# Forgetting attention inside a decoder layer on one core: softmax tiles turned two steps behind their scores, through six buffers, with the per-head work of two engines laid out anew

## The chip, the core and the metric

The kernel runs on one core of one Trainium2 chip. A core has five engines that run their own instruction streams in order and meet through semaphores: PE (TensorE, matrix products), DVE (VectorE), ACT (ScalarE), POOL (GpSimd) and SP (SyncE, which only issues DMAs here). The metric is the device time of one execution in microseconds (us), the median of several runs.

## What is computed

One layer: attention with a forget gate (16 heads of 64, 1024 tokens, width 1024), LayerNorm, then a mixture of 64 small experts with one shared expert, and LayerNorm again. Only the attention bears on the change:

```
proj = x @ w_in                       # q, k, v and one gate logit per head
c = cumsum(log_sigmoid(f_logit + b_f))            # over tokens, per head
logits = q k^T * scale + c[t] - c[s], causal
p = softmax(logits);  o = p @ v;  y = concat(o) @ w_out
```

## The kernel before

Every fp32 product is made of reduced-precision parts: an operand is split into a high part (`_hi`, a cast by ACT) and the rest (`_lo`, a subtraction by DVE that waits for the cast), and `split_matmul` runs three matmuls (lines 80 to 82).

**Value stage.** PE makes the values of all heads in 16 groups `n`, each copied out by ACT and DVE into `v_out` and stored by SP to `v_scratch`. At `n == 9` it also makes the q and k of head 0 (`project(0, half)`, two halves of 512 tokens, 24 matmuls each). The running sums of the gate, `c_hi` and `c_lo`, are ready at `n == 5`; SP stores them after the last group. POOL then waits for these stores before it sets the rows of ones (semaphore `aug`), and SP, ACT, DVE and PE wait for `aug`.

**Head loop.** Head `h` has 8 query tiles of 128 tokens, steps `t` = 0 to 7. The scores of tile `t` span 128(t+1) keys, cut into pieces of up to 512, the 12 slots: one slot for tiles 0 to 3, two for tiles 4 to 7 (slots 4 and 5, 6 and 7, 8 and 9, 10 and 11). Scores land in three PSUM banks in turn (`slot_banks`). Each slot passes:

1. `scores` (PE, lines 817 to 820);
2. `maxima` (DVE, 1548; with two slots also the minimum of their negated maxima, 1552);
3. `exponentials` (ACT, 1193), after the maxima of the whole tile, into `probs[n % 4]`; each is followed by a read of its row sum;
4. `turns` (PE, 847): transposes of 128x128 blocks into one of two banks (`key_banks`, by `u % 2`), after the exponential, and after `turned_low` has read the bank's content of two entries ago;
5. `turned_high` (ACT, 1204), then `turned_low` (DVE, 1559), which give `pt_hi` and `pt_lo`;
6. `weigh_v` (PE, 868): products with the values, once per half of the tiles.

The list `TURNS` has 14 entries `u`: 12 transposes of slots and two `rows` entries, which spread the reciprocals of the row sums over a bank. Slots of tile 7 are turned in step 0 of the next head, all others one step after their scores. Beside this stands work that is done once per head: `project(h + 1)` (PE) in pieces by `PROJECT[t]`, its weights' splitting (`weights_hi` on ACT, 1165, `weights_lo` on DVE, 1500), `take` (both engines read q and k out of PSUM), `low_values` (ACT, 1212), `normalise` (DVE, 1574 and 1578, which frees a key bank) and `reciprocals` (DVE). No scheduler is at work: the order of the code is the order on each engine.

**End.** In head 15 there is nothing to project; ACT and DVE split `w_out` instead (`split_wo`, one piece in each step from 2 to 7, two afterwards), and the last `weigh_v` and the output projection follow.

## Time and profile before

| what | us |
|---|---|
| median of 3 runs (lowest, highest) | 1902.46 (1892.62, 1911.94) |
| the profiled execution | 1887.1 |
| its span, first to last instruction | 1885.4 |
| value stage behind head 0's projection | 104.8 to 145.3 |
| wait between value stage and head 0 | 145.3 to 160.85 |
| heads 0 to 14, up to step 7's maxima of head 14 | 160.85 to 641.6 |
| head 15 up to its last `weigh_v` | 641.6 to 693.8 |
| output projection, routing, experts, last LayerNorm | 693.8 to 1885.4 |

Times of the profile are counted from the span's start. An engine's busy time is the union of its instructions' times; the granted clock is 1.00 at TensorE's upper level (2.4 GHz) and 0.50 at its lower one (1.2 GHz), a mean in between where a stretch saw both.

### The profile page before, as it was taken

How to read it: one execution, taken by the hardware profiler on the slowest of the kernel's cores; microseconds unless marked ns; L12 is line 12 of the kernel's file. 1: busy time of each engine (PE TensorE's matmuls, PEld its weight loads, DVE VectorE, ACT ScalarE, POOL GpSimd, SP SyncE). 2: the span in 40 equal slices, each digit the busy share in tenths (PEclk: the TensorE clock that was granted, in tenths of full speed). 3: DMA queues.
4: the chain of work that ended last, by engine and by line, in shares of the span. 5: the costliest groups of instructions: out<-in, count | busy, mean ns of one | idle time of the engine just before them, and what ended most of it. 6: DMA issues, size and time to landing. Idle time of an engine off the chain costs nothing.

```text
span 1885.4 us, 31807 instructions
## 1 busy us (share of the span) xinstructions
PE 1650.2 (88%) x8302; PEld 1323.5 (70%) x8303; DVE 1200.7 (64%) x2030; ACT 1017.2 (54%) x1672; POOL 474.1 (25%) x486
## 2 busy tenths in 40 slices
PE   7995888888888859989999999999999999999960
PEld 5894666666676648777877777777777777787740
DVE  3212656556565556885566777777776777787836
ACT  3113545554555443333566676766766676777732
POOL 0000000000000000545144444444344443544420
PEclk9998999999999869889999999999999999999995
DMA  5313222212121214264799999998999899999956
GB/s 178 114 68 76 51 51 47 53 39 62 39 62 34 86 62 171 81 236 138 256 299 286 280 302 358 327 282 264 267 301 291 262 317 320 333 339 333 372 135 263
DMA packets 161508, 369.26 MB, mean 196 GB/s; under 512 B 53040, under 2 KB 73520, under 8 KB 161456
## 3 DMA queue, kind: packets, MB, share of 16 engines
q1 hardware_dynamic: 136272, 284.21, 44.2%
q0 software_dynamic: 25184, 84.39, 17.8%
q8 instruction: 28, 0.46, 0.1%
q14 instruction: 24, 0.20, 0.0%
HBM read 294.39 MB, written 65.77 MB: 191 GB/s over the span
## 4 chain that ended last, share of the span: by engine, by line
PE 46%; DVE 19%; issue 11%; DMA 11%; ACT 9%; POOL 2%; DVEq 1%; POOLq 1%; ACTq 1%; SPq 0%
DMA sums_scratch<-ys,sidx 5%; DVE nm L1548 5%; PE bank L969 4%; PE bank L975 4%; PE bank L972 4%; DVE pt_lo L1559 4%; PE out_ps L1027 3%; PE out_ps L1028 3%; DMA x_rows<-rows_scratch,gidx 3%; ACT probs L1193 3%; PE q_ps L959 3%; PE k_ps L1004 2%; PE k_ps L996 2%; PE k_ps L997 2%; PE bank L80 2%
## 5 line engine op out<-in xcount | busy, mean ns | idle before, releaser
L1778 DVE TENSOR_TENSOR gu_lo<-raw_gu,gu_hi 128x1024 fp32r<-128x1024 f32 x260 | 306.8, 1222 | 20.6 <-ACT gu_hi L1297 20.0
L1297 ACT CAST gu_hi<-raw_gu 128x1024 fp32r<-128x1024 f32 x260 | 252.7, 1048 | 0.0
L969 PE MATMUL bank<-gu_hi,xb_hi 128*128 128x512 f32 x576 | 235.0, 408 | 1.4 <-ACT ex L1289 1.3
L972 PE MATMUL bank<-gu_lo,xb_hi 128*128 128x512 f32 x576 | 227.6, 395 | 0.0
L1559 DVE TENSOR_TENSOR pt_lo<-k_ps,pt_hi 128x512 fp32r<-128x512 f32 (+1 forms) x192 | 100.9, 553 | 139.1 <-ACT pt_hi L1204 138.2
L1193 ACT ACTIVATE probs<-bank,nm 128x512 f32<-128x512 f32 (+3 forms) x128 | 73.9, 579 | 191.8 <-DVE nm L1552 107.6
L1778 DVE TENSOR_TENSOR dn_lo<-raw_dn,dn_hi 128x1024 fp32r<-128x1024 f32 x130 | 154.6, 1209 | 0.5 <-ACT dn_hi L1297 0.5
L641 POOL DMA_INDIRECT sums_scratch<-ys,sidx x64 | 114.2, 1784 | 131.4 <-DMA sums_scratch<-ys,sidx 76.8
L975 PE MATMUL bank<-gu_hi,xb_lo 128*128 128x512 f32 x576 | 146.2, 395 | 0.0
L576 POOL IOTA e<- 128x64 f32 x1 | 0.2, 190 | 550.6 <-DVE xs L1578 550.6
L1297 ACT CAST dn_hi<-raw_dn 128x1024 fp32r<-128x1024 f32 x130 | 129.5, 1046 | 0.0
L847 PE MATMUL k_ps<-ident,probs 128*128 128x128 f32 x576 | 94.5, 295 | 38.0 <-DVE pt_lo L1559 31.1
L969 PEld LDWEIGHTS bank<-gu_hi,xb_hi 128*128 128x128 f32 x576 | 109.5, 190 | 25.8 <-issue 2.5
L975 PEld LDWEIGHTS bank<-gu_hi,xb_lo 128*128 128x128 f32 x576 | 108.0, 187 | 26.4
L80 PE MATMUL q_ps<-xt_hi,wqk_hi 128*128 128x512 f32 x256 | 115.2, 450 | 11.9 <-DVE wqk_lo L1500 11.9
L972 PEld LDWEIGHTS bank<-gu_lo,xb_hi 128*128 128x128 f32 x576 | 108.9, 189 | 22.6
L996 PE MATMUL k_ps<-dn_hi,ht_hi 128*128 128x512 f32 x288 | 122.2, 424 | 1.4 <-ACT ht_hi L1326 1.4
L997 PE MATMUL k_ps<-dn_lo,ht_hi 128*128 128x512 f32 x288 | 117.6, 408 | 0.0
L847 PEld LDWEIGHTS k_ps<-ident,probs 128*128 128x128 f32 x576 | 70.9, 150 | 64.9 <-DVE pt_lo L1559 32.2
L959 PE MATMUL q_ps<-ident,x_rows 128*128 128x128 f32 x576 | 85.6, 295 | 29.8 <-DMA x_rows<-rows_scratch,gidx 24.1
L1318 ACT CAST xb_hi<-q_ps 128x1024 fp32r<-128x1024 f32 x72 | 73.1, 1016 | 67.3 <-PE q_ps L959 67.3
L1782 DVE TENSOR_TENSOR xb_lo<-q_ps,xb_hi 128x1024 fp32r<-128x1024 f32 x72 | 88.1, 1224 | 29.7 <-ACT xb_hi L1318 28.2
(268 smaller groups left out, 4123.8 us busy)
## 6 DMA issues: line engine op xcount, KB each, us to landing
raw_gu<-in_moe_w_gate_dram SPq DMA_DIRECT2D x128, 512.0 KB, 6.7
raw_gu<-in_moe_w_up_dram SPq DMA_DIRECT2D x128, 512.0 KB, 8.4
raw_dn<-in_moe_w_down_dram SPq DMA_DIRECT2D x128, 512.0 KB, 6.6
wqk<-in_fox_w_in_dram SPq DMA_DIRECT2D x66, 128.0 KB, 2.4
v_scratch<-v_out SPq DMA_DIRECT2D x32, 256.0 KB, 2.8
va<-v_scratch SPq DMA_DIRECT2D x16, 512.0 KB, 4.7
xs<-in_x_dram SPq DMA_DIRECT2D x8, 512.0 KB, 7.6
wv<-in_fox_w_in_dram SPq DMA_DIRECT2D x4, 1024.0 KB, 7.6
```

The costliest lines, as they stand in the source:

```text
L80: pe.matmul(out, w_hi, m_hi, start=start, stop=False, skip_group_check=True)
L847: i = pe.transpose(bank[:, j * P:(j + 1) * P], probs[n % 4][:, j * P:(j + 1) * P], ident[:])
L959: i = pe.transpose(ps[:, c * P:(c + 1) * P], v[:, c], ident[:])
L969: i = pe.matmul(o3, xb_hi[s][:, c], g_hi[:, :, c], start=c == 0, stop=False, skip_group_check=True)
L972: pe.matmul(o3, xb_hi[s][:, c], g_lo[:, :, c], start=False, stop=False, skip_group_check=True)
L975: i = pe.matmul(o3, xb_lo[s][:, c], g_hi[:, :, c], start=False, stop=c == DC - 1, skip_group_check=True)
L996: pe.matmul(k_ps[:, r], ht_hi[:, c], d_hi[:, c, r], start=c == 0, stop=False, skip_group_check=True)
L997: pe.matmul(k_ps[:, r], ht_hi[:, c], d_lo[:, c, r], start=False, stop=False, skip_group_check=True)
L1193: a.activation(probs[n % 4][:, 0:w], slot_banks[n % 3][:, 0:w], ACT.Exp, bias=nm[:, t:t + 1], accum_out=ssum[par][:, k, t:t + 1]).then_inc ...
L1297: a.copy(hi, raw).then_inc(S[done], 1)
L1559: dve.tensor_tensor(pt_lo[:, at, :], key_banks[u % 2][:, 0:count * P].rearrange("p (j q) -> p j q", q=P), pt_hi[:, at, :], ALU.subtract).t ...
L1778: dve.tensor_tensor(lo, raw, hi, ALU.subtract).then_inc(S[lo_ok], 1)
```

## The change

- `probs` has six buffers in place of four, and `TURNS` and the new `STEP_TURNS` turn every slot two steps behind its scores: tile 6 in step 0 of the next head, tile 7 in step 1.
- On PE the transposes of a step stand ahead of its pieces of projection; the two `weigh_v` move from steps 2 and 5 to 3 and 7.
- On ACT the `turned_high` of a step stand ahead of its `exponentials`. On DVE the `turned_low` still follow the `maxima`.
- The work done once per head is spread over other steps.
- The gate sums are stored during the value stage (`n == 7`), POOL sets the rows of ones without waiting for any store, the second half of head 0's projection follows the value groups, and the weights of head 1 are split there too.

```diff
+PROBS = 6
...
-TURNS = [("turn", -1, 10), ("turn", -1, 11), ("rows", -1, 0), ("turn", 0, 0), ("turn", 0, 1), ("rows", -1, 1)] + [
-    ("turn", 0, n) for n in range(2, 10)]
-
-PROJECT = [((0, 0, 2), (0, 2, 3)), ((0, 3, 7),), ((0, 7, 8),), ((1, 0, 2),), ((1, 2, 4),), ((1, 4, 5),), ((1, 5, 7),), ((1, 7, 8),)]
+TURNS = [("turn", -1, 8), ("turn", -1, 9), ("turn", -1, 10), ("turn", -1, 11), ("rows", -1, 0), ("turn", 0, 0), ("turn", 0, 1),
+         ("turn", 0, 2), ("rows", -1, 1)] + [("turn", 0, n) for n in range(3, 8)]
+
+STEP_TURNS = [(0, 1), (2, 3), (4, 5), (6,), (7,), (8, 9), (10, 11), (12, 13)]
+
+PROJECT = [((0, 0, 3),), ((0, 3, 6),), ((0, 6, 8),), (), ((1, 0, 3),), ((1, 3, 5),), ((1, 5, 7),), ((1, 7, 8),)]
...
-                    probs = [sb(f"probs{i}", [P, BANK], c=b) for i in range(4)]
+                    probs = [sb(f"probs{i}", [P, BANK], c=b) for i in range(PROBS)]
...
-                    nm2 = sb("nm2", [P, 2], c=b)
+                    nm2 = sb("nm2", [P, TT, 2], c=b)
...
+                if n == 7:
+                    sp.wait_ge(S["c_lo_ok"], 2)
+                    sp.dma_start(c_dram[0], c_hi[:].bitcast(F32)).then_inc(S["c_stored"], 16)
+                    sp.dma_start(c_dram[1], c_lo[:].bitcast(F32)).then_inc(S["c_stored"], 16)
...
-            sp.wait_ge(S["c_lo_ok"], 2)
-            sp.dma_start(c_dram[0], c_hi[:].bitcast(F32)).then_inc(S["c_stored"], 16)
-            sp.dma_start(c_dram[1], c_lo[:].bitcast(F32)).then_inc(S["c_stored"], 16)
             sp.wait_ge(S["c_stored"], 32)
+            sp.wait_ge(S["v_ps"], NVC * TT // 2)
+            load_c(sp, 0, 0)
+            copy_halves(sp, 0, 0, 0)
             for i in range(2):
                 sp.wait_ge(v_stored[i], 32 * NVC * TT // 4)
+            load_v(sp, 0, 0)
+            copy_halves(sp, 0, 0, 1)
             sp.wait_ge(S["wqk_lo_ok"], 3)
             load_wqk(sp, 2, 0)
-            sp.wait_ge(S["aug"], 2)
-            for half in range(2):
-                copy_halves(sp, 0, 0, half)
-            load_c(sp, 0, 0)
-            load_v(sp, 0, 0)
...
-            pool.wait_ge(S["v_ok"], NVC * TT // 2)
-            for i in range(2):
-                pool.wait_ge(v_stored[i], 32 * NVC * TT // 4)
-            pool.wait_ge(S["c_stored"], 32)
             pool.wait_ge(S["v_ps"], NVC * TT // 2)
             for par in range(2):
                 g.memset(qk[par][1][DH:K2, :].bitcast(F32), 1.0).then_inc(S["aug"], 1)
...
                     pe.wait_ge(S["c_lo_ok"], 2)
-                    for half in range(2):
-                        project(0, half, range(DC))
+                    project(0, 0, range(DC))
...
-            pe.wait_ge(S["aug"], 2)
+            project(0, 1, range(DC))
 
             def scores(h, par, t):
 
                 q_both, q_ones, k_twice, k_rest = qk[par]
                 if t == 0:
+                    if static(h) and h < 2:
+                        pe.wait_ge(S["aug"], h + 1)
...
-                    for k, (half, c0, c1) in enumerate(PROJECT[t]):
+                    turns(h, par, STEP_TURNS[t], first)
+                    if t == 3 and not first:
+                        weigh_v(h - 1, 1 - par, 1)
+                    if t == 7:
+                        weigh_v(h, par, 0)
+                    for half, c0, c1 in PROJECT[t]:
                         if not last:
                             project(h + 1, half, range(c0, c1))
-                        if t == 0 and k == 0:
-                            turns(h, par, (0, 1), first)
-                    if t == 1:
-                        turns(h, par, (2, 3), first)
-                    elif t == 2:
-                        if not first:
-                            weigh_v(h - 1, 1 - par, 1)
-                        turns(h, par, (4,), first)
-                    elif t == 3:
-                        turns(h, par, (5, 6), first)
-                    elif t == 4:
-                        turns(h, par, (7,), first)
-                    elif t >= 5:
-                        turns(h, par, (2 * t - 2, 2 * t - 1), first)
-                    if t == 5:
-                        weigh_v(h, par, 0)
...
-            turns(HEADS, 0, (0, 1, 2), ends=True)
+            turns(HEADS, 0, (0, 1, 2, 3, 4), ends=True)
             weigh_v(HEADS - 1, 1, 1)
-            turns(HEADS, 0, (5,), ends=True)
+            turns(HEADS, 0, (8,), ends=True)
...
-                if n in (3, 12):
+                if n == 3:
                     for piece in range(2):
-                        weights_hi(n // 12, piece)
+                        weights_hi(0, piece)
...
-                    if not (static(h) and NS * h + n < 4):
-                        act.wait_ge(S["turned_ps"], NS * h + (n - 3))
-                    a.activation(probs[n % 4][:, 0:w], slot_banks[n % 3][:, 0:w], ACT.Exp, bias=nm[:, t:t + 1],
+                    if not (static(h) and NS * h + n < PROBS):
+                        act.wait_ge(S["turned_ps"], NS * h + (n + 1 - PROBS))
+                    a.activation(probs[n % PROBS][:, 0:w], slot_banks[n % 3][:, 0:w], ACT.Exp, bias=nm[:, t:t + 1],
...
+                    for u in STEP_TURNS[t]:
+                        if TURNS[u][0] == "turn" and not (first and TURNS[u][1]):
+                            turned_high(h, u)
                     exponentials(h, par, t)
-                    if t == 0 and not first:
-                        if left > 1:
-                            weights_hi(h + 1, 1)
-                        turned_high(h, 0)
-                        turned_high(h, 1)
+                    if t == 0 and not first and left > 1:
+                        weights_hi(h + 1, 1)
+                    elif t == 1 and not first:
                         take(h, par, 1)
-                    elif t == 1:
-                        turned_high(h, 3)
-                    elif t == 2:
+                        low_values(h - 1, 0)
+                    elif t == 3:
                         if left > 1:
                             take(h + 1, 1 - par, 0)
-                        turned_high(h, 4)
-                    elif t == 3:
                         if not first:
                             low_values(h - 1, 1)
-                        turned_high(h, 6)
-                    elif t == 4:
-                        turned_high(h, 7)
-                    elif t >= 5:
-                        if t == 6 and left > 2:
-                            weights_hi(h + 2, 0)
-                        if t == 7:
-                            low_values(h, 0)
-                        for u in (2 * t - 2, 2 * t - 1):
-                            turned_high(h, u)
+                    elif t == 6 and left > 2:
+                        weights_hi(h + 2, 0)
...
-            act.wait_ge(S["aug"], 2)
+            act.wait_ge(S["v_ps"], NVC * TT // 2)
             for half in range(2):
                 take(0, 0, half)
+                weights_hi(1, half)
+            for i in range(2):
+                act.wait_ge(v_stored[i], 32 * NVC * TT // 4)
...
-            turned_high(HEADS, 0)
-            turned_high(HEADS, 1)
+            for u in range(4):
+                turned_high(HEADS, u)
+            low_values(HEADS - 1, 0)
...
-                    if t == 0 and not first:
-                        if left > 1:
-                            weights_lo(h + 1, 1)
+                    if t == 0 and not first and left > 1:
+                        weights_lo(h + 1, 1)
+                    if t == 2 and not first:
+                        normalise(h - 1, *before_it, 0)
+                    if t == 5 and not first:
+                        normalise(h - 1, *before_it, 1)
+                    for u in STEP_TURNS[t]:
+                        if TURNS[u][0] == "turn" and not (first and TURNS[u][1]):
+                            turned_low(h, u)
+                    if t == 1 and not first:
                         reciprocals(h - 1, 1 - par, 1)
-                        turned_low(h, 0)
-                        turned_low(h, 1)
                         take(h, par, 1)
-                    elif t == 1:
-                        if not first:
-                            normalise(h - 1, *before_it, 0)
-                        turned_low(h, 3)
-                    elif t == 2:
-                        if left > 1:
-                            take(h + 1, 1 - par, 0)
-                        turned_low(h, 4)
-                    elif t == 3:
-                        if not first:
-                            normalise(h - 1, *before_it, 1)
-                        turned_low(h, 6)
-                    elif t == 4:
-                        turned_low(h, 7)
+                    elif t == 3 and left > 1:
+                        take(h + 1, 1 - par, 0)
+                    elif t == 6:
+                        if left > 2:
+                            weights_lo(h + 2, 0)
                         reciprocals(h, par, 0)
-                    elif t >= 5:
-                        if t == 7 and left > 2:
-                            weights_lo(h + 2, 0)
-                        for u in (2 * t - 2, 2 * t - 1):
-                            turned_low(h, u)
...
             for half in range(2):
                 take(0, 0, half)
+                weights_lo(1, half)
...
-            turned_low(HEADS, 0)
-            turned_low(HEADS, 1)
+            for u in range(4):
+                turned_low(HEADS, u)
+            normalise(HEADS - 1, PAIRS - 1, 1, 0)
             split_wo(range(STAGES, DC))
-            normalise(HEADS - 1, PAIRS - 1, 1, 0)```

ACT, second head of the loop body, steps 6 and 7; `probs`, `pt_hi` and `wqk_hi` are the exponentials, the casts of turned blocks and the weights' high parts. Before:

```order
L1193 ACTIVATE probs0,ssum0<-out_ps,nm 128x512 [waits turned_ps,maxed]
L1193 ACTIVATE probs1,ssum0<-bank0,nm 128x384 [waits turned_ps]
L1161 ISA
L1163 ISA [waits wqk_in0]
L1165 CAST wqk_hi<-wqk 128x512 [waits proj]
L1199 REGISTER_ALU
L1204 CAST pt_hi<-k_ps 128x4x128 [waits pv,turned_ps]
...
L1204 CAST pt_hi<-k_ps 128x2x128 [waits pv,turned_ps]
...
L1193 ACTIVATE probs2,ssum0<-bank1,nm 128x512 [waits turned_ps,maxed]
L1193 ACTIVATE probs3,ssum0<-out_ps,nm 128x512 [waits turned_ps]
```

and now:

```order
L1194 CAST pt_hi<-k_ps 128x4x128 [waits pv,turned_ps]
...
L1194 CAST pt_hi<-k_ps 128x128 [waits pv,turned_ps]
L1178 REGISTER_ALU
L1183 ACTIVATE probs2,ssum0<-out_ps,nm 128x512 [waits turned_ps,maxed]
L1183 ACTIVATE probs3,ssum0<-bank0,nm 128x384 [waits turned_ps]
...
L1155 CAST wqk_hi<-wqk 128x512 [waits proj]
...
L1194 CAST pt_hi<-k_ps 128x4x128 [waits pv,turned_ps]
...
L1194 CAST pt_hi<-k_ps 128x2x128 [waits pv,turned_ps]
...
L1183 ACTIVATE probs4,ssum0<-bank1,nm 128x512 [waits turned_ps,maxed]
L1183 ACTIVATE probs5,ssum0<-out_ps,nm 128x512 [waits turned_ps]
```

The casts of a step moved ahead of its exponentials, and are those of the tile before (slots 4 and 5 in step 6, not 6 and 7).

DVE, end of step 7 of that head and steps 0 and 1 of the next; `pt_lo` is `turned_low`, `nm` the maxima. Before:

```order
L1500 TENSOR_TENSOR wqk_lo<-wqk,wqk_hi 128x512 [waits wqk_hi_ok]
L1559 TENSOR_TENSOR pt_lo<-k_ps,pt_hi 128x4x128 [waits turned_hi]
L1559 TENSOR_TENSOR pt_lo<-k_ps,pt_hi 128x3x128 [waits turned_hi]
L1546 ISA
L1548 TENSOR_REDUCE nm<-bank0 128x1 [waits score]
...
L1500 TENSOR_TENSOR wqk_lo<-wqk,wqk_hi 128x512 [waits wqk_hi_ok]
L1567 TENSOR_TENSOR rsum<-ssum0 128x4 [waits exped]
L1569 RECIPROCAL rec0<-rsum 128x4 [waits rec_step]
...
L1559 TENSOR_TENSOR pt_lo<-k_ps,pt_hi 128x4x128 [waits turned_hi] x2
```

and now:

```order
L1542 TENSOR_TENSOR pt_lo<-k_ps,pt_hi 128x4x128 [waits turned_hi]
L1542 TENSOR_TENSOR pt_lo<-k_ps,pt_hi 128x2x128 [waits turned_hi]
L1529 ISA
L1531 TENSOR_REDUCE nm<-bank0 128x1 [waits score]
...
L1484 TENSOR_TENSOR wqk_lo<-wqk,wqk_hi 128x512 [waits wqk_hi_ok]
...
L1542 TENSOR_TENSOR pt_lo<-k_ps,pt_hi 128x4x128 [waits turned_hi]
...
L1542 TENSOR_TENSOR pt_lo<-k_ps,pt_hi 128x3x128 [waits turned_hi]
L1529 REGISTER_ALU
L1531 TENSOR_REDUCE nm<-bank1 128x1 [waits score]
...
L1542 TENSOR_TENSOR pt_lo<-k_ps,pt_hi 128x4x128 [waits turned_hi] x2
```

The first split of the weights left step 7; the second one in step 0 still stands ahead of that step's `turned_low`, which is now that of tile 6, and tile 7's follows in step 1.

SP, from the last store of values to the first loads of head 0. Before:

```order
L376 DMA v_scratch<-v_out 128x512
L380 DMA c_scratch<-c_hi 16x1024 [waits c_lo_ok]
L381 DMA c_scratch<-c_lo 16x1024
L301 DMA wqk<-in_fox_w_in_dram 128x4x64 [waits v_stored1,wqk_lo_ok,v_stored0,c_stored]
...
L321 DMA q_ones<-q_both 64x512 [waits aug,ev_hi]
L322 DMA k_twice<-k_twice 64x512
...
L307 DMA k_rest<-c_scratch 2x1024
L310 DMA va<-v_scratch 128x8x128
```

and now:

```order
L383 DMA v_scratch<-v_out 128x512
L310 DMA k_rest<-c_scratch 2x1024 [waits v_ps,c_stored]
L324 DMA q_ones<-q_both 64x512 [waits ev_hi]
L325 DMA k_twice<-k_twice 64x512
L313 DMA va<-v_scratch 128x8x128 [waits v_stored1,v_stored0]
L324 DMA q_ones<-q_both 64x512 [waits copied,ev_hi]
```

The stores of the gate sums are gone from here, and the loads that head 0's first scores need come first.

## Rows read from the trace of the kernel before

**Rows 1.** The page's line on DVE's and PE's busy time.

```profile
PE 1650.2 (88%) x8302; PEld 1323.5 (70%) x8303; DVE 1200.7 (64%) x2030; ACT 1017.2 (54%) x1672; POOL 474.1 (25%) x486
```

**Rows 2.** Stretches of the program: length, then busy times, clock, DMA.

```profile
core 0: us, PE busy (x) PEld busy (x) DVE busy (x) ACT busy (x) POOL busy (x), PEclk, DMA share, GB/s
145.30:160.85 15.55, 0.00 (x0) 0.03 (x1) 3.45 (x5) 4.22 (x6) 2.39 (x4) 0.65 0.41 96
160.85:188.50 27.65, 24.28 (x111) 18.26 (x112) 10.35 (x25) 10.64 (x31) 0.00 (x0) 0.89 0.23 57
188.50:641.60 453.10, 392.38 (x2074) 301.02 (x2073) 272.81 (x576) 234.22 (x615) 0.00 (x0) 0.97 0.20 49
641.60:693.80 52.20, 29.19 (x120) 22.04 (x118) 31.23 (x57) 26.61 (x57) 0.00 (x0) 0.63 0.25 86
```

**Rows 3.** Two heads of the loop, then 0.8 us at the start of one.

```profile
382.50:415.00 32.50, 28.64 (x149) 22.04 (x149) 19.60 (x43) 16.77 (x44) 0.00 (x0) 0.95 0.20 49
415.00:447.40 32.40, 27.51 (x148) 20.97 (x148) 19.39 (x41) 16.77 (x44) 0.00 (x0) 1.00 0.20 49
...
386.00:386.80 0.80, 0.80 (x3) 0.61 (x3) 0.00 (x0) 0.78 (x2) 0.00 (x0) 0.50 0.41 89
```

**Rows 4.** Timeline, steps 6 and 7: start, length, instruction [idle before <- releaser].

```profile
410.26 0.39 PE L81 MATMUL q_ps<-xt_lo,wqk_hi 128*128 128x512 f32 x1
410.47 0.68 DVE L1548 TENSOR_REDUCE nm<-out_ps 128x1 f32<-128x512 f32 x1
410.49 0.39 PE L82 MATMUL q_ps<-xt_hi,wqk_lo 128*128 128x512 f32 x1
...
411.06 0.55 DVE L1548 TENSOR_REDUCE nm<-bank 128x1 f32<-128x384 f32 x1
...
411.84 0.69 ACT L1193 ACTIVATE probs<-out_ps,nm 128x512 f32<-128x512 f32 x1 [2.04 <-DVE nm L1552]
...
412.67 0.50 PE L817 MATMUL out_ps<-k_twice,q_both 128*128 128x512 f32 x1 [0.66 <-ACT probs L1193]
...
413.07 0.61 ACT L1165 CAST wqk_hi<-wqk 128x512 fp32r<-128x512 f32 x1
...
413.58 0.86 ACT L1204 CAST pt_hi<-k_ps 128x512 fp32r<-128x512 f32 x2
...
414.21 1.02 DVE L1559 TENSOR_TENSOR pt_lo<-k_ps,pt_hi 128x512 fp32r<-128x512 f32 x2 [2.40 <-ACT pt_hi L1204]
414.95 0.99 PE L847 MATMUL k_ps<-ident,probs 128*128 128x128 f32 x7 [0.71 <-DVE pt_lo L1559]
415.14 0.68 DVE L1548 TENSOR_REDUCE nm<-bank 128x1 f32<-128x512 f32 x1
...
417.32 0.50 PE L80 MATMUL q_ps<-xt_hi,wqk_hi 128*128 128x512 f32 x1 [0.48 <-DVE wqk_lo L1500]
```

**Rows 5.** Timeline, from the value stage to the first scores.

```profile
145.93 0.69 DVE L1531 TENSOR_TENSOR v_out<-bank,v_out 128x512 fp32r<-128x512 f32 x1 [5.06 <-ACT v_out L1179]
146.65 0.81 SPq L376 DMA_DIRECT2D v_scratch<-v_out  x2
...
150.73 1.95 POOL L566 MEMSET q_ones<- 2x1024 f32 x2 [146.49 <-DMA c_scratch<-c_lo]
152.71 0.59 ACT L1184 ACTIVATE q_both<-q_ps 64x512 fp32r<-64x512 f32 x1 [6.81 <-POOL q_ones L566]
...
160.85 0.44 PE L817 MATMUL bank<-k_twice,q_both 128*128 128x128 f32 x1 [15.58 <-DMA k_rest<-c_scratch]
```

**Rows 6.** DMA issues there: KB each, median us to landing.

```profile
k_twice<-k_twice SPq DMA_DIRECT2D x2, 128.0 KB, 2.7
```

**Rows 7.** Timeline, end of head 15.

```profile
684.36 0.68 ACT L1193 ACTIVATE probs<-out_ps,nm 128x512 f32<-128x512 f32 x1
...
686.62 1.06 ACT L1217 CAST wo_hi<-wo 128x1024 fp32r<-128x1024 f32 x1
...
690.69 2.36 DVE L1584 TENSOR_TENSOR wo_lo<-wo,wo_hi 128x1024 fp32r<-128x1024 f32 x2 [0.25 <-ACT wo_hi L1217]
...
693.79 0.77 PE L868 MATMUL out_ps<-pt_hi,va 128*128 128x512 f32 x1 [2.83 <-DVE heads_sum L1574]
```

More of the change, by code:

```diff
@@ L833, in bank_free @@
                     assert u < 2
-                    pe.wait_ge(S["turned_lo"], NS * h + (TURNS[12 + u][2] + 1 - NS))
+                    pe.wait_ge(S["turned_lo"], NS * h + (TURNS[len(TURNS) - 2 + u][2] + 1 - NS))
             def turns(h, par, us, first=False, ends=False):
@@ L846, in turns @@
                         for j in range(SLOTS[n][2] // P):
-                            i = pe.transpose(bank[:, j * P:(j + 1) * P], probs[n % 4][:, j * P:(j + 1) * P], ident[:])
+                            i = pe.transpose(bank[:, j * P:(j + 1) * P], probs[n % PROBS][:, j * P:(j + 1) * P], ident[:])
                         i.then_inc(S["turned_ps"], 1)
@@ L1519, in _ @@
             for n in range(NVC * TT // 2):
-                if n in (3, 12):
+                if n == 3:
                     for piece in range(2):
-                        weights_lo(n // 12, piece)
+                        weights_lo(0, piece)
                 if n and n % (TT // 2) == 0 and n // (TT // 2) + 1 < NVC:
@@ L1532, in _ @@
                                   ALU.subtract).then_inc(S["v_ok"], 1)
-            dve.wait_ge(S["aug"], 2)
             def take(h, par, half):
@@ L1547, in maxima @@
                     one = len(OF_TILE[t]) == 1
-                    dve.tensor_reduce(nm[:, t:t + 1] if one else nm2[:, k:k + 1], slot_banks[n % 3][:, 0:SLOTS[n][2]], AX_X, ALU.max,
+                    dve.tensor_reduce(nm[:, t:t + 1] if one else nm2[:, t, k:k + 1], slot_banks[n % 3][:, 0:SLOTS[n][2]], AX_X, ALU.max,
                                       negate=True).then_inc(S["maxed"] if one else S["max_step"], 1)
@@ L1551, in maxima @@
                     dve.wait_ge(S["max_step"], TT * h + 2 * (t - 3))
-                    dve.tensor_tensor(nm[:, t:t + 1], nm2[:, 0:1], nm2[:, 1:2], ALU.min).then_inc(S["maxed"], 1)
+                    dve.tensor_tensor(nm[:, t:t + 1], nm2[:, t, 0:1], nm2[:, t, 1:2], ALU.min).then_inc(S["maxed"], 1)
             def turned_low(h, u):
@@ L1630, in _ @@
             reciprocals(HEADS - 1, 1, 1)
-            turned_low(HEADS, 0)
-            turned_low(HEADS, 1)
+            for u in range(4):
+                turned_low(HEADS, u)
+            normalise(HEADS - 1, PAIRS - 1, 1, 0)
             split_wo(range(STAGES, DC))
-            normalise(HEADS - 1, PAIRS - 1, 1, 0)
             def heads_lo(t):
```

## The prediction

> **What bounds the kernel now.** I read the busy shares first: PE 88% and DVE 64% of the span [rows 1]. No engine is full, so the stretches decide. Four of them are touched: a wait of 15.55 us with PE idle; head 0; fourteen head-to-head distances, 453.1 us or 32.4 us each; head 15 with 52.2 us [rows 2]. The rest is left alone.
>
> In one head of 32.4 us at full clock PE is busy 27.5 us, DVE 19.4 and ACT 16.8 [rows 3]; PE idles 4.9 us. What ends its waits is read from the timeline of two steps [rows 4]. From the maxima of step 6 (410.47) to those of step 7 (415.14) DVE and ACT work one after the other: two maxima and the minimum 1.37 us, until the exponential starts at 411.84; both exponentials to 413.07, 1.23; the weights' cast to 413.58, 0.51; the casts of the turned blocks until DVE can begin at 414.21, 0.63; DVE's two subtractions to 415.14, 0.93. The sum is 4.67 us, the whole step. DVE idles 2.40 us of it and ACT 2.04, each for the other, and PE, with about 3.0 us of work in the step, stands at 412.67, 414.95 and 417.32 for one or the other. So the bound is a ring: maxima(t), exponentials(t), turned_high, turned_low, maxima(t+1), on two in-order engines.
>
> **The ring goes.** In the new order ACT casts blocks of two tiles ago while DVE is at the maxima, and DVE's turned_low finds its cast done. A step then costs an engine its own work: for DVE in step 6 1.37 + 0.93, with weights and a reciprocal 3.1 us; ACT about the same. PE becomes the longest. Its issue time per head is a little under the 27.5 us busy: a matmul that is followed at once takes 0.23 us of its 0.39 [rows 4], and one ahead of a wait counts in full, 0.16 us for some four or five places, so 26.8.
>
> **What PE still waits for.** I walked one head of the new order by hand with the durations of rows 4, from PE's step 7 as time 0. DVE is 2.4 us behind there, since weights_lo has moved to step 6 and waits for a cast that stands behind that step's exponentials. Maxima of step 7 end at 3.85, exponentials at 5.65, turned_low of slots 6 and 7 at 4.5 and 4.85. PE reaches the next head at 4.0, and its transposes need those two banks: waits of 0.3 and 0.3. In step 0 ACT does two casts (6.6), an exponential (7.1), the weights' cast (7.75); DVE's weights_lo waits for that one (8.5), and only then come turned_low of slots 8 and 9 (9.1, 9.6). PE wants these banks for tile 7 at 7.95 and waits 1.2 us, the largest gap. In step 1 DVE's take waits for ACT (14.0), normalise in step 2 ends at 15.9, and PE's transpose of step 3, which needs its bank, waits 0.5 us. The second weigh_v of a head is then free to start. Steps 4 to 7 show no wait of PE: the score of a tile's second slot comes some 3 us after that of the tile before, and maxima, minimum and exponential take 2.2 of them. The waits make 2.3 us, of which 0.2 overlap; 26.8 + 2.1 = 28.9, and I add 0.3 for semaphore hops that I left out: **29.2 us a head**. Fourteen of them save 14 x (32.4 - 29.2) = **44 us**. The six buffers cost nothing by themselves. Bounds: no wait at all is the 27.5 us row, 69 us saved; waits twice as long, 30.5 to 31.3 us, save 27 to 15.
>
> **The wait ahead of head 0.** Before, PE ends the value stage at 145.3 and starts scores at 160.85 [rows 2, 5]: the last values are stored at 146.65, then the gate sums, POOL waits for their landing and takes 1.95 us, ACT starts at 152.71, the copies and loads follow. Afterwards half of head 0's projection, 24 x 0.23 = 5.5 us, stands behind the value groups, so these end at 139.8 and the projection at 145.3. Meanwhile ACT and DVE take the first half (to 143), POOL fills its rows (to 141.9), and SP, behind two stores of values (0.81 us), loads the sums and issues the copies at about 143.5; with 2.7 us to landing [rows 6] scores start near 146.5. That is **14.4 us** (11 if the copies queue behind the values' stores, 15.5 at most). The store moved to n = 7 passes SP's queue while groups of 5.8 us run, its sums being long ready: nothing. The splitting of head 1's weights fits between the two takes.
>
> **Head 0** ran at a clock of 0.89 [rows 2] because PE came from a long idle: 0.11 of 27.65 us, 3 us. After an idle of one us I expect the upper level. With 1 us more for its last steps, **4 us** (0 to 5).
>
> **Head 15.** There the ring has one more member pair, the split of w_out: ACT's cast 1.06 us and DVE's subtraction, half of 2.36 [rows 7], stand in it in every step from 2 on. They stay, as DVE waits for the cast behind the exponentials; what leaves is the pair of casts of turned blocks, about 0.9 us in seven steps, 6.3 us. At the end, from the last exponential's end (684.36 + 0.68) to the last weigh_v (693.79) it is 8.7 us [rows 7], with 2.36 us of w_out ahead of normalise. The new tail turns four slots instead of two (two of them can start earlier) and puts normalise first; by the same durations 6.0. So 2.7 us more, **9 us** in all (3 to 12).
>
> **The sum.** 44 + 14.4 + 4 + 9 = 71.4 us, from the profiled 1887.1 to 1815.7. The median of the runs is 1902.46, 15.4 us above the profiled one; I put that down to the rest of the program and subtract from the median: **1831 us**. The difference that a measurement of this kernel can tell from none is about 1%.
>
> **Clock.** At a head's start PE fell to 0.50 for some 3 us after gaps of about a microsecond each, in one of two heads: the means are 0.95 and 1.00 [rows 3]. My walk assumes that this stops. The Trainium skill ("TensorE: Matmul & The Clock Gate", section "A second HAM failure mode: psum-queue depth-cycling") describes short idles between groups of matmuls as enough to make the clock swing. The rows of this trace agree with it, and by it the gaps that I leave at the head's start could keep the swing, the third rival below: 1842 by that rule, 1831 by my walk.
>
> **Rivals.**
> 1. PE is the bound with no gaps of note (my lags of DVE are too long): 27.5 us a head, 69 us in place of 44: 1806. For it: ACT and DVE are under 20 us busy. Against: the 1.2 us gap follows from in-order queues. 0.17.
> 2. A new ring at the head's start: ACT's exponentials of step 7, casts, weights' cast, DVE's weights_lo, turned_low, PE's transposes. If every hop is longer than I took, the head costs 30.5 us and the loop saves 27: 1848. 0.15.
> 3. The clock swing stays, 1.6 us in each pair of heads, seven pairs: 11 us: 1842. The idle that is left is half of that before. 0.12.
> 4. The change doesn't do what it says in the loop (PE's transposes ahead of the projections make it wait for the banks in each step), the loop stays at 32.4, and the rest saves 27: 1875. 0.04.
> 5. Slower. The projections were what PE did while its banks were read; now the transposes come first, and each bank is freed by a turned_low behind the maxima of the step. If each of 8 steps showed the wait of step 1 (1.2 us) and PE ran a quarter of the loop at its lower level, the head would be 26.8 + 9.6 + 3.4 = 39.8 us, 104 us more in the loop, less 27 elsewhere: 1980. It decides from 34.3 us a head, 7.5 us of waits against my 2.4. The rows speak against it: DVE would need to be late by a step each time. 0.03.
>
> The forecast has 0.49. The range runs from 1805 (rival 1) to 1858 (rival 2 with the lower bounds of the smaller terms), and leaves out rivals 4 and 5 and edges of the others. Faster by over 1%: 0.95; within 1%: 0.02; slower: 0.03.
>
> **What would show it.** In the new profile the distance of heads is 29 us, PE busy near 27 of them; DVE's idle ahead of turned_low (2.40 in a step) is near zero, save in step 0; PE's largest wait is for turned_low of slot 8 ahead of the transposes of step 1, near 1.2 us; the first scores stand near 146.5; head 15 is some 9 us shorter. I am wrong if PE waits in steps 4 to 7 for exponentials or banks, if its clock mean falls under 0.95 in the loop, or if the first scores still wait for a DMA issued after 150.

## The result, and the profile after

The changed kernel takes 1795.86 us (median of 4 runs, 1792.89 to 1798.77); the kernel before, timed beside it on the same chip, 1902.33 (4 runs, 1892.62 to 1911.94). The ratio is 0.947, 95% interval 0.943 to 0.951: faster by 106 us, where 71 were predicted. The time lies 9 us below the range. The profiled execution took 1796.52 us, its span 1794.8.

The page's busy line of the changed kernel, which answers to [rows 1]:

```profile
PE 1620.6 (90%) x8302; PEld 1323.3 (74%) x8303; DVE 1201.5 (67%) x2030; ACT 1017.3 (57%) x1672; POOL 465.8 (26%) x486
```

The instruction counts of these engines are the same. DVE and ACT are busy for the same time, but PE for 29.6 us less. Part of that is the granted clock, which was 0.97 in the loop before [rows 2] and is 1.00 now; the rest shows in single heads at 1.00, 27.51 us before [rows 3] against 25.94 and 25.74: a first sign that PE's busy time is not a constant of the work. The windows are cut at the same events as [rows 2], with two single heads below as in [rows 3]; the columns are those of [rows 2]:

```profile
146.40:168.65 22.25, 20.04 (x110) 16.24 (x111) 13.74 (x30) 13.68 (x36) 0.00 (x0) 1.00 0.40 99
168.65:551.80 383.15, 361.94 (x2073) 301.82 (x2072) 273.15 (x575) 235.09 (x618) 0.00 (x0) 1.00 0.24 57
551.80:592.50 40.70, 25.77 (x121) 19.69 (x119) 27.23 (x51) 24.32 (x55) 0.00 (x0) 0.75 0.32 110
...
341.40:368.80 27.40, 25.94 (x151) 21.68 (x150) 19.51 (x43) 16.69 (x44) 0.00 (x0) 1.00 0.24 58
368.80:396.20 27.40, 25.74 (x150) 21.38 (x148) 19.44 (x41) 16.89 (x44) 0.00 (x0) 1.00 0.24 58
```

The fourteen distances are 27.4 us each, not 32.4: 70.0 us. First scores stand at 146.39 and not at 160.85: 14.5. Head 0 takes 22.26 us for 28.13: 5.9. Head 15 to its last weigh_v takes 40.6 us for 51.7: 11.1. From there to the output projection's first matmul (702.56 before, 600.14 after) 1.1 more is saved (before, PE's 512-column matmuls here follow each other at 0.43 us, its lower clock level; after, the first ones do, and from 595.88 on they follow at 0.24), so that this matmul starts 102.4 us earlier. Behind it the code is the same and took 1182.8 us in the one profiled execution and 1194.7 in the other. All twelve profiles of this study, of kernels that do not differ there, lie between 1177.5 and 1197.7: that is the spread of single executions. It is why I compare the medians for the whole and positions in the traces for the parts.

The ring is gone, as two lists of waits show (who waited, for whom: total us, number, longest; `k_ps` is a key bank, `xs` what `normalise` writes). First the kernel before, two heads from 382.5 to 447.4:

```profile
DVE pt_lo L1559 <- ACT pt_hi L1204: 18.3, 9, 2.4
ACT probs L1193 <- DVE nm L1552: 17.6, 8, 2.7
ACT probs L1193 <- DVE nm L1548: 11.3, 7, 2.2
```

The changed kernel, two heads from 341.4 to 396.2:

```profile
ACT pt_hi L1194 <- PE k_ps L848: 15.6, 14, 2.1
...
ACT probs L1183 <- DVE nm L1535: 2.0, 2, 1.1
...
ACT probs L1183 <- DVE nm L1531: 1.6, 2, 0.8
PE k_ps L848 <- DVE xs L1561: 1.6, 2, 0.8
...
PE k_ps L848 <- DVE pt_lo L1542: 1.4, 3, 0.6
DVE pt_lo L1542 <- ACT pt_hi L1194: 1.3, 3, 0.6
```

DVE waited 18.3 us for ACT's casts and ACT 28.9 us for maxima; now it is 1.3 and 3.6. What ACT waits for now is PE, the engine that bounds. The timeline shows it from step 6 of a head to step 1 of the next (columns as in [rows 4]):

```profile
354.58 0.67 DVE L1531 TENSOR_REDUCE nm<-out_ps 128x1 f32<-128x512 f32 x1
...
355.16 0.48 PE L83 MATMUL q_ps<-xt_hi,wqk_hi 128*128 128x512 f32 x1
...
355.33 0.75 ACT L1194 CAST pt_hi<-k_ps 128x512 fp32r<-128x512 f32 x2 [0.99 <-PE k_ps L848]
355.48 0.39 PE L84 MATMUL q_ps<-xt_lo,wqk_hi 128*128 128x512 f32 x1
...
355.70 0.40 PE L85 MATMUL q_ps<-xt_hi,wqk_lo 128*128 128x512 f32 x1
...
355.95 0.89 DVE L1542 TENSOR_TENSOR pt_lo<-k_ps,pt_hi 128x512 fp32r<-128x512 f32 x2
...
355.97 0.71 ACT L1183 ACTIVATE probs<-out_ps,nm 128x512 f32<-128x512 f32 x1
...
356.62 0.39 PE L818 MATMUL bank<-k_twice,q_both 128*128 128x512 f32 x1
...
357.87 0.69 DVE L1484 TENSOR_TENSOR wqk_lo<-wqk,wqk_hi 128x512 fp32r<-128x512 f32 x1 [1.03 <-ACT wqk_hi L1155]
...
358.56 0.66 DVE L1531 TENSOR_REDUCE nm<-bank 128x1 f32<-128x512 f32 x1
...
363.38 0.69 DVE L1484 TENSOR_TENSOR wqk_lo<-wqk,wqk_hi 128x512 fp32r<-128x512 f32 x1 [2.24 <-ACT wqk_hi L1155]
...
363.99 1.15 DVE L1542 TENSOR_TENSOR pt_lo<-k_ps,pt_hi 128x512 fp32r<-128x512 f32 x2
364.73 1.12 PE L848 MATMUL k_ps<-ident,probs 128*128 128x128 f32 x8 [0.61 <-DVE pt_lo L1542]
...
371.62 0.43 PE L848 MATMUL k_ps<-ident,probs 128*128 128x128 f32 x2 [0.83 <-DVE xs L1561]
```

In step 6 the cast (355.33) comes ahead of the exponential (355.97), and DVE takes pt_lo at 355.95 without a wait. At 364.73 stands the predicted gap of step 1: the `turned_low` of step 0 (363.99) comes late, since the split of weights ahead of it waited 2.24 us for a cast; PE waits 0.61 us, not 1.2. At 371.62 is step 3's wait for normalise.

The handover in the changed kernel, which answers to [rows 5]:

```profile
140.69 1.95 POOL L566 MEMSET q_ones<- 2x1024 f32 x2 [136.45 <-PE bank L85]
141.14 0.59 ACT L1174 ACTIVATE q_both<-q_ps 64x512 fp32r<-64x512 f32 x1
...
143.94 0.58 SPq L325 DMA_DIRECT2D k_twice<-k_twice  x1
...
146.39 0.30 PE L818 MATMUL bank<-k_twice,q_both 128*128 128x128 f32 x1 [0.30 <-DMA k_twice<-k_twice]
```

### The profile page after: what moved, and what is told of

Its sections match the earlier page's. It is cut to its first block, busy times and chain, and to the rows that moved or that the text cites. A ratio compares the mean times of both kernels' runs of the same rounds, so it can differ in the third digit from the quotient of the medians.

```text
span 1794.8 us, 31900 instructions
## 1 busy us (share of the span) xinstructions
PE 1620.6 (90%) x8302; PEld 1323.3 (74%) x8303; DVE 1201.5 (67%) x2030; ACT 1017.3 (57%) x1672; POOL 465.8 (26%) x486
## 4 chain that ended last, share of the span: by engine, by line
PE 55%; DVE 12%; issue 12%; DMA 11%; ACT 6%; POOL 1%; DVEq 1%; another core or an unknown queue 1%; POOLq 1%; ACTq 0%; SPq 0%
DMA sums_scratch<-ys,sidx 6%; PE bank L959 4%; PE bank L962 4%; PE bank L965 4%; PE out_ps L1017 4%; PE out_ps L1018 3%; DMA x_rows<-rows_scratch,gidx 3%; PE q_ps L949 3%; PE out_ps L869 3%; ACT probs L1183 2%; PE k_ps L994 2%; PE k_ps L986 2%; PE k_ps L987 2%; DVE nm L1531 2%; PE bank L83 2%
## 5 line engine op out<-in xcount | busy, mean ns | idle before, releaser
L1194 ACT CAST pt_hi<-k_ps 128x512 fp32r<-128x512 f32 (+1 forms) x192 | 85.9, 482 | 118.2 <-PE k_ps L848 117.9
L848 PE MATMUL k_ps<-ident,probs 128*128 128x128 f32 x576 | 89.5, 284 | 27.7 <-DVE xs L1561 13.9
L1542 DVE TENSOR_TENSOR pt_lo<-k_ps,pt_hi 128x512 fp32r<-128x512 f32 (+1 forms) x192 | 100.7, 552 | 14.1 <-ACT pt_hi L1194 12.3
L83 PE MATMUL q_ps<-xt_hi,wqk_hi 128*128 128x512 f32 x256 | 108.9, 426 | 0.0
L1017 PE MATMUL out_ps<-gu_hi,xo 128*128 128x512 f32 x248 | 104.1, 420 | 4.9 <-DVE xo L1775 4.9
## 6 DMA issues: line engine op xcount, KB each, us to landing
wqk<-in_fox_w_in_dram SPq DMA_DIRECT2D x66, 128.0 KB, 2.4
```

Source lines behind the costliest of these rows:

```text
L83: pe.matmul(out, w_hi, m_hi, start=start, stop=False, skip_group_check=True)
L1017: pe.matmul(o3, xo[:, c], g_hi[:, :, c], start=c == 0, stop=False, skip_group_check=True)
L1542: dve.tensor_tensor(pt_lo[:, at, :], key_banks[u % 2][:, 0:count * P].rearrange("p (j q) -> p j q", q=P), pt_hi[:, at, :], ALU.subtract).t ...
```

## The experiments

Each was timed against the kernel before on the same chip; the ratio stands with its 95% interval. "A head" is the mean of the fourteen distances in its trace. The kernel before had medians of 1890.1, 1892.9 and 1893.6 us in these comparisons (9, 13 and 7 executions), where it had 1902.3 above. The times in us that I expected were built on that one or on the changed kernel's 1796, so some 10 us of what they were off by is this; ratio and head are the measures to compare. Line numbers shift from kernel to kernel, the names do not.

**1. The handover alone** (kernel before, with the new value stage and start of head 0).

```
+                if n == 7:  # SP: both c_dram stores go here
...
-            pool.wait_ge(S["c_stored"], 32)
...
+            project(0, 1, range(DC))   # PE, behind the value groups
```

> The kernel before with only the changes between the value stage and head 0 (stores of the gate sums at n = 7, rows of ones without a wait for stores, second half of head 0's projection behind the value groups, head 1's weights split there). My theory, that this part is additive: the first scores stand at 146.4 us of the span, as in the changed kernel (160.85 before), and head 0 runs at full clock, some 3 us shorter; the loop keeps its 32.4 us a head; 1885 us, 17 to 18 less than before. The rival, that the early start is only worth something with the new loop (head 0 ends when its own ring ends): under 10 us less, 1893 or more.

0.985 (0.982 to 0.988), median 1863.6. First scores at 147.38, head 0 25.69 us, a head 32.38. The handover is worth 13.5 us. Head 0 is 2.4 us shorter with the same waits of PE, at a clock of 0.99 in place of 0.89, so that part is the clock. Neither touches the loop; its clock was 0.99 here and 0.97 in the kernel before, with the same 32.4 us a head, so the loop's clock did not set the head either. The output projection starts 17.7 us earlier; the time fell by 26.5. Of the difference 5.3 lie in the rest of the program, whose code is the same, and 3.0 in that the median of the kernel before was above its profiled execution: spread, not the edit. The 1885 us that I expected started from 1902.5; 12 of the 21 us by which it was missed are the other median of the kernel before.

**2. Casts ahead of the exponentials, one tile behind** (kernel before, ACT's queue only; nm2 gets a column pair for each tile).

```
+                    for u in ((0, 1), (3,), (4,), (6,), (7,), (8, 9), (10, 11), (12, 13))[t]:
+                        if not (first and TURNS[u][1]): turned_high(h, u)
                     exponentials(h, par, t)
...                  # the turned_high calls behind it are gone
```

> The kernel before, four buffers and one tile behind, with ACT's casts of the turned blocks ahead of the step's exponentials and nothing else moved (the minima's inputs get a place per tile). Theory A, the order alone breaks the ring: 29 us a head or less, 1850 us or less. Theory B, one tile behind the cast now waits for transposes that stand behind the projection on PE, a ring of its own (second score of a tile, 1.4 us of projection, transposes 0.8, casts and first exponential 1.9, less 0.5 in which PE scores the first slot: some 3.6 to 4.6 us a step in the heavy steps): 31 to 33 us a head, 1880 to 1910 us, no clear gain. I hold B.

1.009 (1.006 to 1.012), a head 34.08. Its waits, 350 to 418:

```profile
ACT pt_hi L1204 <- PE k_ps L847: 35.3, 14, 3.7
```

The casts stand at the head of ACT's queue, but their transposes stand behind the projection in PE's. The exponentials wait behind the casts. I had expected 31 to 33 us a head.

**3. Transposes ahead of the projections, one tile behind** (kernel before, PE's queue only, where the transpose of step 2 passes a `weigh_v` too; nm2 as in experiment 2).

```
                     scores(h, par, t)
+                    turns(h, par, ((0, 1), (2, 3), (4,), (5, 6), (7,), (8, 9), (10, 11), (12, 13))[t], first)
                     for half, c0, c1 in PROJECT[t]: ...
```

> The kernel before, four buffers and one tile behind, with only PE's transposes moved ahead of the step's projection; ACT's casts stay behind the exponentials (the minima's inputs get a place per tile). If the ring of DVE and ACT (maxima, exponentials, casts, turned_low) sets the head, which in the kernel before did not wait for the transposes at the casts: no more than 0.5 us a head, 31.9 to 32.4 us, 1880 to 1892 on this chip. If PE's order by itself is worth what it was in the pair with ACT's order (4.8 us between the two kernels one tile behind): 29 us a head or less.

1.015 (1.013 to 1.017), a head 34.09. Its waits, 350 to 420:

```profile
ACT probs L1182 <- DVE nm L1541: 20.1, 9, 2.7
DVE pt_lo L1548 <- ACT pt_hi L1193: 17.5, 9, 2.4
...
PE k_ps L847 <- DVE pt_lo L1548: 11.1, 8, 3.3
```

The ring stays whole, and PE now meets its busy banks before it has the projection to do (11.1 us of waits for `turned_low` in two heads, 2.8 in the kernel before): that is rival 5's mechanism, at 1.7 us a head. I had expected no loss.

**4. Both orders, one tile behind, four buffers** (experiments 2 and 3 together).

> As the previous kernel, and on PE the transposes ahead of the step's projection as well: still four buffers and one tile behind. Theory A (the order on ACT and PE is what counts, the second tile of lag is not needed): 27.5 to 29.5 us a head, 1830 to 1860 us. Theory C (a lag of two is needed: one tile behind, PE's transposes wait for the exponentials of the tile just scored, and these for the casts): 30 to 31.5 us a head, 1865 to 1885 us. By adding up exponentials 1.2, transposes 0.8 and casts 1.0 for a step I get 3.0 to 3.4 us in steps 5 to 7, near PE's own 3.3, so I lean to A, near 29.

0.973 (0.969 to 0.976), a head 29.31, as I had leaned to (near 29). Two edits that each lose 1.7 us a head save 3.1 together. The new lag of two tiles and the rest of the layout give 1.9 more; no run separates these two. What PE still waits for in the fourteen heads of this experiment is `normalise` (18.9 us) and `turned_low` (24.5 us), against 10.7 and 10.0 in the changed kernel.

**5. Four buffers in the changed kernel.**

```
-PROBS = 6
+PROBS = 4
```

> The changed kernel with four buffers of probabilities in place of six. An exponential then waits for the transposes of the slot four before it, which in this order stand ahead of the casts that ACT has already done. Theory: the buffers do nothing, 27.4 us a head and 1796 us, within 0.3%. Rival: the lag of two tiles needs six buffers, the exponentials wait on PE: over 28.5 us a head, 1812 us or more.

0.944 (0.941 to 0.948), median 1783.4, a head 27.39 against 27.37: no gain and no loss by the buffers. The median is 12 us under the 1796 that I expected; on that chip the kernel before stood 12 us lower too.

**6. Casts behind the exponentials in the changed kernel.**

```
+                    exponentials(h, par, t)
                     for u in STEP_TURNS[t]: ... turned_high(h, u)
-                    exponentials(h, par, t)
```

> The changed kernel with ACT's casts back behind the step's exponentials; two tiles behind, six buffers and PE's order stay. If the ring is made by the order on ACT and DVE (maxima, exponentials, casts, turned_low, one after the other, whatever tile the casts are of): 31 to 32.5 us a head in place of 27.4, 1850 to 1870 us. If the lag of two tiles alone breaks it: 27.4 to 28 us a head, 1796 to 1805 us. I hold the first.

0.977 (0.973 to 0.981), a head 30.92. Its waits, 350 to 412:

```profile
ACT probs L1183 <- DVE nm L1535: 16.5, 9, 2.3
DVE pt_lo L1542 <- ACT pt_hi L1194: 16.2, 12, 2.0
```

Two tiles of lag do not break the ring if ACT's order is the old one: of the 5.0 us a head 3.5 are gone.

**7. Projection ahead of the transposes in the changed kernel** (the PROJECT loop moved ahead of turns and weigh_v).

> The changed kernel with the projection ahead of the transposes on PE, as it was before. If PE's order matters because the casts wait for the transposes and the exponentials for the casts (ACT idles behind 1.4 us of projection in each step): 29 to 31 us a head, 1820 to 1845 us. If two tiles of lag give room enough: 27.4 to 28, 1796 to 1805 us. I hold the first, near 29.

1.005 (1.002 to 1.008), a head 35.80. Its waits from 350 to 421 and a window, in which the clock is 0.91 (0.93 in the whole loop):

```profile
ACT pt_hi L1194 <- PE k_ps L848: 29.3, 14, 2.9
```

```profile
350.00:410.00 60.00, 49.09 (x248) 38.77 (x246) 31.92 (x67) 27.34 (x73) 0.00 (x0) 0.91 0.21 49
```

The whole gain is lost by this order alone. The mechanism is that of experiment 2: casts at the head of ACT's queue, whose transposes come late. I had expected 29 to 31 us a head; so late transposes cost far more than I thought, even with two tiles of lag. Of the 8.4 us a head more than in the changed kernel, 3.2 are busy time of PE (407.2 us in the fourteen heads for 361.9), in which the lower clock has its part, and the rest is waiting.

**8. DVE's split of the next weights behind turned_low in step 0.**

```
-                    if t == 0 and not first and left > 1:
-                        weights_lo(h + 1, 1)
                     for u in STEP_TURNS[t]: ... turned_low(h, u)
+                    if t == 0 and not first and left > 1:
+                        weights_lo(h + 1, 1)
```

> The changed kernel with DVE's split of the weights in step 0 moved behind that step's turned_low. PE's wait ahead of the transposes of step 1 (0.61 us in the changed kernel's trace) goes, and with it up to 0.6 us a head, 9 us: 1787 us, if no later wait takes its place; 1796 if the split then delays maxima and normalise of steps 1 and 2 by as much as PE gained, so that the wait of step 3 (0.8 us) grows.

0.942 (0.938 to 0.946), median 1781.0, a head 26.52, 0.85 under the changed kernel, where I had expected up to 0.6. PE's waits for xs and pt_lo in two heads, 340 to 393:

```profile
PE k_ps L848 <- DVE xs L1561: 1.6, 2, 0.8
...
PE k_ps L848 <- DVE pt_lo L1542: 0.2, 1, 0.2
```

Step 3's wait stays, that for pt_lo falls from 1.4 to 0.2 in two heads.

**9. The same, with weigh_v ahead of the transpose in step 3** (on PE, one call moved).

> As the previous kernel, and in step 3 the products with the values stand ahead of the transpose of slot 1, which waited 0.8 us for normalise. If the 3.1 us of products only hide that wait: another 0.8 us a head, 1775 us. If ACT, whose exponential of tile 3 stands behind the cast of slot 1, becomes 3 us later and the lag runs on into steps 4 and 5: no gain or a loss, 1787 to 1810 us. I lean to the second, a small loss.

0.955 (0.951 to 0.958), a head 28.32: 1.8 us worse than experiment 8, the loss that I leaned to (median 1806.4 in my 1787 to 1810). The values keep PE busy while DVE normalises, but the transpose behind them comes late, ACT's cast and the exponential behind it with it, and the next scores wait for that one. Its waits, 340 to 397:

```profile
ACT pt_hi L1194 <- PE k_ps L848: 17.4, 12, 3.6
...
PE bank L818 <- ACT probs L1183: 4.0, 2, 2.0
```

A 0.8 us wait was traded for one of 2.0.

**10. Experiment 8, with normalise ahead of the maxima in step 2.**

```
+                    if t == 2 and not first:
+                        normalise(h - 1, *before_it, 0)
                     maxima(h, t)
...
-                    if t == 2 and not first:
-                        normalise(h - 1, *before_it, 0)
```

> The kernel with the later split, and DVE's normalise of step 2 ahead of that step's maxima, so that it frees PE's bank for step 3 earlier (0.8 us of waiting there). If that wait is the last in the chain there: 0.5 us a head less than 26.5, 26.0, some 7 us, 1774 us beside 1781. If the maxima of step 2, 1.3 us later, delay tile 2's exponential and PE's transposes, nothing or a loss of some us.

0.940 (0.936 to 0.944), median 1779.98, a head 26.07. In the traces its heads are shorter than those of the changed kernel and of experiment 8. The ratio's interval just meets that of the changed kernel and overlaps that of experiment 8 (0.938 to 0.946), so the evidence is the head's distance, 1.3 us less than in the changed kernel in each of fourteen and 0.45 less than in experiment 8. One head of it, then PE's two longest waits in it:

```profile
360.00:386.07 26.07, 25.49 (x149) 21.35 (x148) 19.48 (x42) 16.49 (x44) 0.00 (x0) 1.00 0.25 61
```

```profile
361.92 0.43 PE L848 MATMUL k_ps<-ident,probs 128*128 128x128 f32 x2 [0.37 <-DVE xs L1561]
...
378.58 0.98 PE L848 MATMUL k_ps<-ident,probs 128*128 128x128 f32 x7 [0.21 <-DVE pt_lo L1542]
```

## Why the prediction was off

The bound, the direction and the smaller terms were right; the size of the loop's term was not. **The step that failed is the one that set PE's own work: "Its issue time per head is a little under the 27.5 us busy", 26.8 us, and with it the bound "no wait at all is the 27.5 us row".** The loop term was 44 us and measured 70.0, 29.2 us a head against 27.37: PE's own work was 25.8 us and not 26.8, and the term beside it, 2.1 and 0.3 us of waits, was 1.6. The prediction also contradicts itself here: with 26.8 us of work the case of no waits would be 26.8 us a head, some 1797 us in all, and not the 27.5 us row that made 1806.

- **PE's own work, 26.8.** It measured 25.94 and 25.74 us in two heads, and 25.49 in experiment 10's. A whole head of experiments 8 and 10, waits included (26.52 and 26.07), is shorter than what I took for PE's work alone. This is 0.96 of the 1.83 us by which the head was missed. An estimate of where it comes from can be made from rows. A 512-column matmul followed at once gives way after 0.22 to 0.23 us (355.48 to 355.70), while one ahead of a wait counts its full 0.39: 0.17 more. The first one behind transposes holds its successor back for 0.32 (355.16 to 355.48), 0.09 more, and one behind a stop for 0.34 (in the kernel before, 417.32 [rows 4] to 417.66). So a stop adds, by this estimate, some 0.25 us that the busy column books as work. I counted four or five stops at 0.16. The head of [rows 3] from 415.00 has seven waits of 0.4 us or more, the changed one at 341.40 two. Five stops less are 1.3 us of the 1.6 to 1.8 that PE's busy time fell by; the remainder I can't assign. Experiments 8 and 10 bear the price out. The fourteen heads of experiment 8 have 14 waits for `turned_low` less than those of the changed kernel (6 for 20), one a head, and as many for `normalise`; PE's busy time falls from 361.94 to 358.29 us, 0.26 a head. Experiment 10 has as many waits as experiment 8 and halves those for `normalise` (11.1 to 4.6 us); there PE's busy time stays. Experiment 8's fourteen heads, then experiment 10's:

```profile
168.84:540.08 371.24, 358.29 (x2073) 301.04 (x2072) 275.55 (x575) 235.13 (x618) 0.00 (x0) 1.00 0.25 59
```

```profile
169.40:534.37 364.97, 358.61 (x2074) 301.05 (x2072) 274.52 (x575) 232.53 (x618) 0.00 (x0) 1.00 0.25 60
```

- **The waits, 2.1 and 0.3 for hops.** PE idles 1.46 and 1.66 us in the two heads. Their places were right, their sizes not: step 1 0.61 for 1.2, step 3 0.76 and 0.83 for 0.5, the start of the next head 0.1 and 0.2 for 0.6. My walk had DVE 2.4 us late at step 7; it is 1.94 (score at 356.62, maximum at 358.56). That is 0.84 of the miss. Experiment 8 shows that the cause named for step 1 was the right one: with the split moved, 0.6 us of waiting a head is gone and the head is 0.85 shorter, more than the wait itself, as a stop's own price would have it.
- **The ring.** Read rightly as what bounded the loop, but a reader could take from the prediction that the lag breaks it. Experiments 2, 3, 4, 6 and 7 show what does: ACT's casts ahead of its exponentials and PE's transposes ahead of its projections, both. With one tile of lag either alone loses (34.08 and 34.09 for 32.37), and both together give 3.1 of the 5.0 us. With two tiles PE's order alone gives 1.4 (30.92), ACT's alone loses 3.4 (35.80). "The six buffers cost nothing" held, and they bring nothing either.
- **The wait ahead of head 0, 14.4.** Measured 14.5; first scores forecast near 146.5, found at 146.39; the copies were issued at 143.35 to 143.94 (143.5 forecast).
- **Head 0, 4.** Measured 5.9. Experiment 1 splits it: the clock gives 2.4 (3 forecast), the new loop the other 3.4 (1 forecast); which of its edits does it in head 0 no run shows.
- **Head 15, 9.** Measured 11.1, inside its 3 to 12. The clock there rose from 0.63 to 0.75, which the sum did not count, and no run separates it from the order. Two of its waits I had not named: PE's 3.15 us for normalise in step 3, and ACT's 2.23 us for w_out's first load, both in the changed kernel's timeline:

```profile
560.75 0.44 PE L848 MATMUL k_ps<-ident,probs 128*128 128x128 f32 x2 [3.15 <-DVE xs L1561]
...
562.34 1.04 ACT L1207 CAST wo_hi<-wo 128x1024 fp32r<-128x1024 f32 x1 [2.23 <-DMA wo<-in_fox_w_out_dram]
```

- **Subtracting from the median.** It came out better: with the measured terms, 1902.46 less 14.5, 5.9, 70.0, 11.1 and 1.1 is 1799.9, 4 us from the median after; from the profiled 1887.1 it would have been 1784.5, 11 us from it. No more than spread decides this: the same kernel's medians in the experiments were 1890.1 to 1893.6, between the two.
- **Two sums.** 14 x (32.4 - 29.2) is 44.8 (44.3 with the unrounded 453.1 / 14), and the upper end of the range, rival 2 with the lower bounds 11, 0 and 3, is 1861 and not 1858. Neither bears on the result.

Of the rivals, the first (PE bounds, 1806) came nearest, with 0.17. Its mechanism isn't what happened: the waits that it denied are there, and the floor of 27.5 that it shared with my forecast was the error. So no case of mine reached below 1806, and the range was too high at its low end. The second (30.5 a head) was wrong: the chain at the head's start costs little. The third (the clock swing stays) was wrong: the granted clock is 1.00 in both heads and in the whole loop. The Trainium skill's passage on short idles ("TensorE: Matmul & The Clock Gate", section "A second HAM failure mode: psum-queue depth-cycling") says that in one kernel PE idled so often between groups of matmuls that the clock swung between its levels. The trace does not show that for the idles left here: gaps of 0.61 and 0.83 us in a head left the clock at its upper level of 2.4 GHz. In the loops of experiments 2, 3 and 7, whose longest waits of PE were 1.7, 3.3 and 2.8 us, the mean was 0.96, 0.95 and 0.93; that of experiment 6, with one of 1.9, was 0.99 (1.00 from 350 to 410, 0.94 from 410 to 470), and the kernel before and experiment 1, with the same loop and waits of up to 1.3 in the same places, had 0.97 and 0.99. So the longest gap alone doesn't tell it. The fourth did not occur. The fifth, slower from 34.3 us a head, did not occur in this kernel either, but I held it too unlikely for the neighbourhood that the change lives in: experiments 2, 3 and 7 stand at 34.08, 34.09 and 35.80, and my expectations for all three were too good.

## What to carry to other kernels

Where in-order engines pass work in a ring, write for each step the order of all their queues beside each other: a consumer put first is only as early as its producer's place in the other queue, and one half of such a change can be a loss where both halves gain. Busy time of a pipelined engine taken from a stretch with stops in it is no floor for the same work without them; the start-to-start distance of instructions that follow at once, times their number, should be nearer (an inference from the rows here; no forecast was made with it). And after the largest wait is gone, look at the once-per-head work that stands ahead of what PE waits for: two such moves, of one instruction group each, gave 1.3 us a head.

## What was unexpected

- A stop of PE costs more than its idle time: removing a wait of 0.61 us shortened the head by 0.85 (experiment 8), of which 0.26 was busy time of PE, with the same instructions.
- The same loop, with its waits in the same places, was granted a mean clock of 0.97 in one execution (kernel before) and 0.99 in another (experiment 1), and took 32.4 us a head in both.
- The rest of the program, from the output projection on, with the same instructions in every kernel here, took between 1177.5 and 1197.7 us in twelve single executions: 1% of the whole, as large as what some of these experiments measure.
